# Eight experts in an order found on the chip, three of them with 64 token slots instead of 96

## What is computed

```
logits = h @ router_w + router_b
top_val, top_idx = top_k(logits, 2)          # two experts a token
combine = sum(one_hot(top_idx, 8) * softmax(top_val)[..., None], axis=-2)
for e in range(8):
    out = out + combine[..., e:e+1] * ((silu(h @ w1[e]) * (h @ w3[e])) @ w2[e])
```

## Time and profile before

| | us |
|---|---|
| median of 3 runs | 1945.97 (1945.91 to 1948.18) |
| span of the profiled execution, first to last instruction | 1944.6 |
| PE busy in the span | 1900.7 (98%) |
| matmuls of the expert stream, start of first and of last | 1023.8 and 1925.6 |
| the profiled execution's own time beside its span | the page gives none |

### The profile page before, as it was taken

How to read it: one execution, slowest core, us unless ns; L and a number is a source line. 1 busy time by engine, 2 the same in 40 slices (tenths; PEclk the granted TensorE clock), 3 DMA queues, 4 the chain that set the end, 5 groups by cost and what they waited for, 6 DMA issues and landing times.

```text
span 1944.6 us, 48442 instructions
## 1 busy us (share of the span) xinstructions
PE 1900.7 (98%) x22336; PEld 1386.6 (71%) x22337; DVE 603.1 (31%) x1194; ACT 449.6 (23%) x759; POOL 409.3 (21%) x126
## 2 busy tenths in 40 slices
PE   6999999999999999999999999999999999999997
PEld 4875888898888888968986666666666666666664
DVE  4355332253632545475541011110211111120112
ACT  4357322243222224465440000100000000000001
POOL 2400444435546454304530000000000000000000
PEclk8999999999999999999999999999999999999999
DMA  8352332226353655303589999999999999999990
GB/s 343 133 197 85 111 101 95 89 86 238 132 193 133 238 224 185 130 23 131 174 311 384 403 408 382 377 381 408 398 375 397 387 408 380 380 393 401 409 375 25
DMA packets 70144, 506.60 MB, mean 261 GB/s; under 512 B 7793, under 2 KB 8049, under 8 KB 9265
## 3 DMA queue, kind: packets, MB, share of 16 engines
q1 hardware_dynamic: 69552, 501.08, 66.3%
q0 software_dynamic: 384, 2.36, 0.3%
HBM read 502.36 MB, written 1.05 MB: 259 GB/s over the span
## 4 chain that ended last, share of the span: by engine, by line
PE 82%; issue 9%; POOL 5%; DMA 1%; DVE 1%; ACT 1%; SPq 0%; DVEq 0%; POOLq 0%; ACTq 0%
PE bank L1525 30%; PE bank L1537 14%; PE bank L937 10%; PE bank L939 10%; PE bank L938 10%; POOL w_lo L583 5%; DMA start_slab<-in_w_mod 1%; PE pv_bank L1288 1%; PE turned_pair L1270 1%; PE bank L972 1%; PE bank L1246 0%; PE bank L1539 0%; PE bank L1251 0%; PE turned_pair L1511 0%; PE bank L1511 0%
## 5 line engine op out<-in xcount | busy, mean ns | idle before, releaser
L1525 PE MATMUL bank<-moe_slab,HE 128*32 128x256 f32 x10752 | 592.8, 379 | 1.3 <-DVE GT L2847 1.3
L1525 PEld LDWEIGHTS bank<-moe_slab,HE 128*32 128x32 f32 x10752 | 348.7, 110 | 231.2 <-DVE GT L2847 1.8
L583 POOL TENSOR_TENSOR w_lo<-slab,w_hi 128x2048 fp32r<-128x2048 f32 (+3 forms) x88 | 369.0, 4196 | 540.3 <-ACT w_hi L1742 540.3
L937 PE MATMUL bank<-H_HI,w_hi 128*128 128x512 f32 (+1 forms) x912 | 321.6, 353 | 0.4 <-POOL H_LO L851 0.3
L938 PE MATMUL bank<-H_LO,w_hi 128*128 128x512 f32 (+1 forms) x912 | 319.6, 350 | 0.0
L939 PE MATMUL bank<-H_HI,w_lo 128*128 128x512 f32 (+1 forms) x912 | 319.5, 350 | 0.0
L1537 PE MATMUL bank<-moe_slab,GE 128*32 128x256 f32 x4032 | 299.8, 379 | 0.0
L1539 PE MATMUL bank<-moe_slab,GE 128*32 128x256 f32 x1344 | 299.1, 379 | 0.0
L1537 PEld LDWEIGHTS bank<-moe_slab,GE 128*32 128x32 f32 x4032 | 166.6, 110 | 115.0
L2844 DVE TENSOR_TENSOR GT<-SE,bank 128x256 f32<-128x256 f32 x56 | 23.6, 421 | 631.8 <-ACT SE L2082 631.8
L2080 ACT ACTIVATE SE<-bank 128x256 f32<-128x256 f32 x56 | 21.4, 383 | 772.0 <-PE bank L1525 772.0
(11 more groups left out here) (289 smaller groups left out, 2022.9 us busy)
## 6 DMA issues: line engine op xcount, KB each, us to landing
moe_slab<-in_moe_up SPq DMA_DIRECT2D x224, 1024.0 KB, 7.3
moe_slab<-in_moe_w SPq DMA_DIRECT2D x112, 1024.0 KB, 7.2
slab<-in_w_in SPq DMA_DIRECT2D x38, 1024.0 KB, 4.9
slab<-in_ffn_w SPq DMA_DIRECT2D x30, 1024.0 KB, 4.9
row_slab<-in_w_mod_rows SPq DMA_DIRECT2D x28, 1024.0 KB, 7.1
start_slab<-in_w_mod SPq DMA_DIRECT2D x8, 1024.0 KB, 17.1
slab<-in_w_proj SPq DMA_DIRECT2D x8, 1024.0 KB, 4.8
slab<-in_w_out SPq DMA_DIRECT2D x8, 1024.0 KB, 4.9
```

The costliest lines, as they stand in the source:

```text
L583: engine.tensor_tensor(lo, raw, hi.bitcast(F32), ALU.subtract).then_inc(done, 1)
L937: mm(out, lhs[0], rhs[0], start=start, stop=False)
L1525: ins = mm(outs[t // 2][32 * b:32 * b + 32, 256 * (t % 2):256 * (t % 2) + 256], rows[t], w[:, 256 * b:256 * b + 256], start=first and t != ...
```

## The change

On the chip the experts are ranked by their token counts (`order` on DVE, new; expert 0 always comes first, its key is set above all counts). Position p of the stream then takes the expert of rank `RANK_AT[p]`. Ranks 0 to 4 keep 96 slots, ranks 5 to 7 get 64; in counting from one, the positions with 64 slots are 2, 5 and 8. SP reads the expert of a position into a register and computes the addresses of its slabs from it. A position with 64 slots has matmuls for two groups of 32 tokens instead of three, with its own versions of the layout of the down product, the silu, the gate and the weighting. The gathers are five instead of four: position 1 alone right after `route`, then 2 and 3, 4 and 5, 6 and 7, and 8 alone, each from step 5 of positions 1, 3, 5 and 7. An expert with more tokens than its slots would go to the overflow passes. The ring, its 14 places, the order of slabs inside an expert and their 336 transfers stay.

```diff
+RANK_AT = (0, 5, 1, 2, 6, 3, 4, 7)
+WIDE = 5
+SLOTS_AT = [SLOTS if rank < WIDE else 64 for rank in RANK_AT]
+GATHERS = ((0,), (1, 2), (3, 4), (5, 6), (7,))
+PLACE_AT = (0, 1, 2, 0, 1, 2, 3, 0)
...
+            def expert_at(p):
+                sp.wait_ge(order_ready, 1)
+                return sp.value_load(ORDER[0:1, p:p + 1], min_val=0, max_val=N_EXPERTS - 1)
...
             def stream_load(k):
-                src, row = (a["moe_up"], (4 * n + i) * P) if kind == "up" else (a["moe_w2"], (2 * n + i) * P)
-                sp.dma_start(moe_slab[k % MOE_RING][:].rearrange("p k n -> p (k n)"), src[row:row + P, :])\
+                p, g = divmod(n, GROUPS)
+                src, each = (a["moe_up"], 4) if kind == "up" else (a["moe_w2"], 2)
+                row = (each * g + i) * P
+                if p:
+                    if p not in expert_of:
+                        expert_of[p] = expert_at(p)
+                    rows = src[bass.ds(expert_of[p] * (GROUPS * each * P) + row, P), :]
+                else:
+                    rows = src[row:row + P, :]
+                sp.dma_start(moe_slab[k % MOE_RING][:].rearrange("p k n -> p (k n)"), rows)\
...
             def token_groups(outs, rows, w, first, last):
-                for t in range(3):
+                for t in range(len(rows)):
...
+            def narrow_column_groups(out, rows, w, first, last):
+                for half in range(2):
+                    for q in range(4):
+                        b = 2 * half + q // 2
+                        ins = mm(out[32 * q:32 * q + 32, 256 * half:256 * half + 256], rows[q % 2],
+                                 w[:, 256 * b:256 * b + 256], start=first and half == 0, stop=last,
+                                 skip_group_check=True)
...
+            def order():
+                link(v.tensor_copy(KEY[:], COUNTF[:]))
+                link(v.memset(KEY[:, 0:1], 2.0 * S))
+                mine = KEY[:].unsqueeze(2).to_broadcast([P, 8, 8])
+                other = KEY[:].unsqueeze(1).to_broadcast([P, 8, 8])
...
+                placed(ORDERF[:], const("iota")[:, 0:8])
+                v.tensor_copy(ORDER[:], ORDERF[:]).then_inc(order_ready, 1)
+                placed(COUNT_AT[:], COUNTF[:])
...
+                for to, of in ((W_AT, W), (POS_AT, POS)):
+                    for t in range(2):
+                        placed(to[:, t, 0:8], of[:, t, 0:8])
...
             def stream():
                 for n in range(STEPS):
                     e, g = divmod(n, GROUPS)
-                    if e % 2 and e + 1 < N_EXPERTS and g == GATHER_AT:
+                    if n == 0:
+                        order()
+                    gather = next_gather(e) if g == GATHER_AT else None
+                    if gather:
```

More of the change, by code:

```diff
@@ L1561, in down_slab, with wait_tokens_out, scatter_quarter @@
                     k = 2 * i + kk
[L1562 to L1563 removed]
+                    first, last = g == 0 and k == 0, g == GROUPS - 1 and k == 3
+                    rows = [GE[:, n % 2, t, 32 * k:32 * k + 32] for t in range(groups)]
+                    if groups == 3:
+                        ins = column_groups(down, rows, w[:, kk, :], first, last)
+                    else:
+                        ins = narrow_column_groups(down[0], rows, w[:, kk, :], first, last)
                 ins.then_inc(slab_used, 1)
[L1566 to L1570 removed]
+            def wait_tokens_out(e, n, groups=3):
+                need = (1, 1, 2, 3) if groups == 3 else (1, 2, 2, 3)
+                pe.wait_ge(ytok_lo, 3 * e + need[n])
+            def scatter_quarter(n, out, slots=SLOTS):
                 for c in range(2):
                     col = P * (2 * n + c)
[L1573 to L1574 removed]
+                    mm(out[:, S * c:S * c + S], YTOK_HI[0:slots, col:col + P], SCATTER[0:slots], start=True,
+                       stop=False)
+                    ins = mm(out[:, S * c:S * c + S], YTOK_LO[0:slots, col:col + P], SCATTER[0:slots], start=False,
+                             stop=True)
                 ins.then_inc(scattered, 1)
@@ L2092, in token_high_parts, with narrow_token_high_parts @@
                 af(YTOK_HI[:, 768:1024], YLAST[:], ACT.Copy, scale=weight).then_inc(ytok_hi, 1)
+            def narrow_token_high_parts(e):
+                weight = SLOT_W[0:64, e % 2:e % 2 + 1]
+                hi = YTOK_HI[0:64, :].rearrange("p (a b n) -> p a b n", a=2, b=2)
+                act.wait_ge(slot_w_ready, e + 1)
+                af(hi[:, :, 0, :], down[0][0:64, :].rearrange("p (a n) -> p a n", a=2), ACT.Copy, scale=weight)\
+                    .then_inc(ytok_hi, 1)
+                for half in range(2):
+                    act.wait_ge(ylast_ready, 3 * e + 2 + half)
+                    af(hi[:, half, 1, :], YMOVED[:, 256 * half:256 * half + 256], ACT.Copy, scale=weight)\
+                        .then_inc(ytok_hi, 1)
             def last_token_high_parts():
@@ L3016, in constants @@
     put("pick", p[:, None] % 32 == f)
+    put("rank_at", np.array(RANK_AT)[None, :])
+    put("spare", SLOTS - np.array(SLOTS_AT)[None, :])
     put("fold", (p[:, None] // 64 == f // 2 % 2) & (p[:, None] % 32 == 2 * (f // 4) + f % 2))
```

174 lines of the change are left out of this document (119 added, 55 removed).

## The result

The changed kernel takes 1885.3 us in the median of 4 runs (1883.38 to 1887.5), against 1946.94 (1945.91 to 1948.18) for the kernel before on the same chip: a ratio of 0.9683, 95% interval 0.967 to 0.9697. The forecast of 1884 was right, in part by luck: two of its terms were off by some 5 us each and cancelled. The profiled execution took 1883.7 us with a span of 1881.9.

What follows compares the result with a forecast made beforehand. PE bounds the kernel, transfers close behind; from position 2 landings set the end: 1132.0 plus 284 x 2.57 = 729.9, last narrow slab 1.7, tail 18.6, sum 1882.2; plus 1.4, say 1884 us. Range 1856 to 1916.

Steps and rivals of the forecast that it cites:

- The bound: Whole stream: PE sets the pace before the change; with it, slabs land one behind the other from position 2 on.
- Narrow slabs: Positions 2, 5 and 8: 16 matmuls a slab instead of 24, so 1.73 us on PE instead of 2.59.
- Slabs landed at position 2: Start of position 2, about 1132.0: 54 slabs issued, two on the way, 52 landed, leaving 284 to land.
- The rate: Transfers from position 2 on: 2.57 us a slab, 408 GB/s, so 284 slabs take 729.9 us.
- The rival at the start's rate: Transfers from position 2 on run at 2.48 us a slab, as at the kernel's start: 1858 us; chance 0.16.
- PE's waits: Narrow positions 2, 5 and 8, most in the last two: PE waits some 47 us in all for landings.
- two wide positions put back some five of the 14 places: Wide positions between narrow ones: 43 to 45 slabs land in each while 42 are used; ring never full again.
- the transfers never rest: From position 2 to the end: transfers run without a pause, DMA share 1.00, no slice below 395 GB/s.
- The start: First gather, one expert instead of two, 96 columns per matmul instead of 192: 1.3 us gained.
- Ranking and addresses: Ranking on DVE, 5.5 to 7 us, hidden ahead of step 0's gate; SP's register addresses hidden: nothing for either.
- The tail: From the last matmuls to the end of the span: 18.6 us, with 1 us to either side.
- The clock rival: Narrow positions: PE's clock falls to 1.2 GHz, a narrow slab takes 3.45 us, up to 2055 in all; chance 0.03.

Runs made afterwards that it cites:

- e4: Changed kernel, but from position 2 on a down slab's transfer brings only its first half (512 KB), with the same matmuls: 1848.36 us, ratio 0.9495.
- e3: Changed kernel with 64 slots at all eight positions, tokens beyond an expert's 64th left out: 1869.05 us.
- e9: Changed kernel with the first gather taking position 1's tokens twice, 192 columns a matmul instead of 96: 1883.62 us, ratio 0.9678.
- e1: Changed kernel with constant slab addresses, experts in the order the ranking gives, instead of register addresses: 1884.96 us, ratio 0.9679.
- e7: Changed kernel with SP allowed to run only 7 slabs ahead of PE, not 14, the 14 places kept: 1912.21 us.
- e10: The changed kernel once more, unedited, beside the run with the wide first gather on one chip: 1888.83 us, ratio 0.9698.
- e6: Changed kernel with its three narrow positions moved from 2, 5 and 8 to 6, 7 and 8: 1908.62 us.
- e8: Changed kernel with 64 slots everywhere and the second group of 32 tokens multiplied only in the first up or down term: 1869.39 us.
- e2: Changed kernel with only positions 2 and 8 narrow, the fifth wide again: 1896.23 us, ratio 0.973.
- e5: Changed kernel with 96 slots at all eight positions; ranking, register addresses and five gathers stay: 1951.43 us, ratio 1.0024.

## Why the prediction was right, and where not

**The bound, shown.** PE paces the stream up to position 2 and the landings pace it from there to the end. e4 takes the landings away and PE's work ends 36.5 us earlier; e3 takes 181 us of PE's work away and the last landing comes 14.8 us earlier.

**Narrow slabs, right.** A wide slab is 48 matmuls and a narrow one 32 (the prediction counted half of each; the ratio of two thirds is what entered). In e4, where nothing waits, position 2 takes 78.5 us: 72.5 by the prediction, 2.4 for a scatter, and 4 x 0.86 = 3.4 because four of the up slabs in this stretch belong to the wide position behind it.

**Slabs landed at position 2: missed by two.** The step took 54 for issued and 52 for landed at 1132.0. In the trace 53 were issued by then and 50 had landed, the 50th at 1130.62 (the 287 slabs from 1132 in e4's expectation are one too many). I took two to be on the way; 7.3 us to landing over 2.59 us a slab already says nearly three. And PE came to position 2 at 1134.1, 2.1 us late, almost one slab.

**The rate: 2.57 us a slab came out nearly right, by two errors that cancel.** 286 slabs landed between 1130.62 and 1860.37: 2.552 us each. Two slabs more cost 5.1 us, 286 x 0.018 gave 5.1 back, and the 50th landing lay 1.4 us ahead of 1132.0: hence 1860.4 against 1861.9. The rate was read from windows with a share of 1.00, and it was still not the most that the transfers can do. In those windows some three slabs were outstanding, that is issued and not yet landed; with a deep queue they moved 419 to 420 GB/s at a share of 1.01. The rival at the start's rate was right that a deep queue moves more. At 419 GB/s a slab is 1.0486 / 0.419 = 2.50 us, and 286 of them would have ended 14 us earlier. They did not, because a slab has landed only with the last of its 16 parts, and eight parts run ahead of the others (last section): while 419 GB/s moved, slabs landed each 2.546 us (100th to 250th). The head start of the early parts comes back at the end: in the last 16 us 175 GB/s moved, which is 16 x (419 - 175) / 419 = 9.3 us, most of the 14. So 2.57 stood on a rate of the transfers that was too low and on no allowance for parts that land unevenly. Of the page of the Trainium skill that was weighed, "DMA: Bandwidth & Descriptors", Specifications: its 358 GB/s for a core, half of 716 for a pair of cores, is far below what every stretch of 1200 to 1650 us shows, where one core ran alone.

**PE's waits: 38 to 40 us, predicted 47.** They grow from position to position, as argued: 5.6, 14.2, 17.9. The forecast had PE's own work ending at 1817, against a last slab at 1863.6. e4 shows 1825.88: its first slab is 2.3 us behind that of the changed kernel, its position 1 is 1.3 us longer, and the changed kernel itself came to position 2 2.1 us late; the other 3 us are spread over the positions and were not split. The step said that two wide positions put back some five of the 14 places. They did: 6 slabs had landed and were not yet used at 1440, and 7 at most from position 3 on, at 1764, one of them in use; the kernel before holds 11 to 13. But the other places were taken too, by slabs on the way. So SP waits for PE in 1640 to 1780, 29 times before up slabs alone, and the transfers rest at 1740 to 1770, for about 30 x (419 - 395) / 419 = 1.7 us. Eight slabs were on the way there, but the parts that run ahead had only two or three left. That the transfers never rest was wrong by this much.

**The start: missed, and in sign.** I took 1.3 us gained. The gather of 96 columns starts a pair of matmuls each 0.22 us, as that of 192 does in e9's and the old trace, so half the columns gain nothing (in e1 and e7, where the clock holds, the first silu comes 14.34 us behind the gather's start, in the kernel before 14.38). It began 0.9 us earlier than before, and then the clock fell to half: the pair at 1022.35 takes 0.62 us instead of 0.39, and step 0's silu came at 1035.14, 0.7 us behind the 1034.43 of the kernel before. The term was 1.3 - (-0.7) = 2.0 us too good, which is nearly all of the 2.1 us by which position 2 came late.

**Ranking and addresses: nothing, right.** The ranking's last instruction ends at 1029.8 and DVE then idles for 6.05 us until the gate. For an address SP has a MOVE of 29 ns and register work of 46, and e1 and the changed kernel differ by 0.3 us.

**The tail: 19.6, predicted 18.6,** at the edge of its bounds. PE waits 1.41 us for `YTOK_LO` at 1864.82, behind the two copies in series that the prediction named without a price; the kernel before waits 0.62 there. In e1 and e10, which end their last slab within 1 us of the changed kernel, the tail takes 22.8: there the clock falls 3.8 us behind the last slab, in the changed kernel 13.3 us behind it. The prediction's 1 us to either side does not cover that. The end of the run lies 1.8 us behind the span, not 1.4.

**The clock rival** did not come in the profiled run. PE's granted clock is 1.00 from 1050 to 1850, in the narrow positions too, behind 48 waits of up to 1.4 us. In e10, the same kernel, it came once, for 3.4 us in position 2, behind a wait for a landing (a row of PE's timeline, and a window):

```profile
1209.92 2.73 PE L1572 MATMUL bank<-moe_slab,HE 128*32 128x256 f32 x32 [1.96 <-DMA moe_slab<-in_moe_up]
...
1210.90:1214.40 3.50, 3.50 (x40) 1.47 (x36) 0.87 (x2) 0.39 (x1) 0.00 (x0) 0.51 1.01 421
```

It did so once each in e3 and e6, behind waits of 2.01 and 2.15 us; ten other waits of over 1.9 us in e3, e6, e7, e9 and e10 were followed by no fall. The price was small: e10's last landing is at 1860.53, that of the changed kernel at 1860.37. In the Trainium skill, "TensorE: Matmul & The Clock Gate", the section on HAM oscillation has matmuls at half clock behind waits for transfers of some 3 to 5 us. No wait here is that long, so these runs do not test it. e8 shows that the clock falls often when PE has still less to do.

## What to carry to other kernels

When the bound engine is relieved, the time moves only as far as the next bound, and that one has to be priced at the pace at which whole slabs land under a deep queue. Neither the rate at a shallow queue (2.57 us a slab) nor that of the bytes at a deep one (2.50) is that pace (2.55). Light stages are worth most where they stand early and among heavy ones, so that a ring can refill and the transfers never rest: the same three narrow positions gave 23 us less at the end of the stream. A gather that gets smaller need not get shorter, and a fall of PE's clock in it can make the stage behind it start later than before.

## What the runs showed of the hardware

**A full DMA share has more than one rate.** With some three slabs of 1 MiB outstanding 402 to 410 GB/s moved at a share of 1.00 or 1.01, with eight to eleven 419 to 420 at 1.01, and in e7 with six 420. The number of slabs is not all: 395 moved with eight outstanding (1740 to 1770), and 405 with between six and seven on average in e2 (1450 to 1550). There the eight parts of a slab that run ahead had 2.4 and 3.2 slabs left on average, in the stretches of 418 to 420 about four and more. What the engines do in the time that a deeper queue saves, no run tells.

**SP's issue is held when the queue is long.** In the changed kernel and in e1 an issue takes up to 6.5 and 7.1 us, against 0.33 normally. In the trace this happens when 11 or 12 slabs are outstanding, the one being issued counted, and never are there more than 12, though the ring has 14. 12 x 2.55 = 30.6 us is also nearly the longest time to landing, 31.0. In e7 and e5, with at most seven and six outstanding, no issue takes over 0.71 us. The ring's last two places are not idle for that: in the wide positions they hold slabs that have landed, and SP waits for PE 60 times before slabs in 1300 to 1460 because all 14 are taken. What two places fewer would cost was not tried.

**Eight of sixteen parts of a slab land late.** Each slab signals 16 completions. In the trace of the changed kernel eight of them run ahead, and the time from the first to the last grows to between 14 and 19 us in the last 60 slabs; before the change it was 2.2 us in the median and 3.6 at most, and in e4, where the transfers rest, 2.5 and 6.0. PE's instruction fetches are a suspect: the stream has 113 of their packets in the changed kernel, 89 in e3 and 51 in e8, and the lag at the end is 16.5, 17.4 and 10.8 us. The lag falls with the fetches from e3 to e8, but not from the changed kernel to e3, so the cause stays open. Its price at the end of the changed kernel is the 9.3 us above; on average the 16 parts of the last slab land 8.6 us before its last one. In e3 that average is 8.3, in e8 5.1: 3.2 of the 4.3 us by which e8's last landing comes before e3's.

**PE's clock fell with PE hardly idle.** In the first gather, of 96 columns, the granted clock goes to 0.5, that is to 1.2 GHz, in eight of the ten traces that have it: for 3.4 us in the changed kernel, e2, e3, e6 and e10, for 6.8 in e4, e5 and e8. In e1 and e7 it holds 1.00, and so it does with 192 columns in the kernel before and in e9, at the same pace of 0.22 us a pair. Before the fall in the changed kernel PE had gone from 512 columns a matmul to 96, after an idle of 0.32 us. e9 has a fall of 3.4 us at 1735.55, at the end of its gather of 96 columns for position 8 and with no wait ahead of it; outside e8 no gather of 192 columns has one. From the start of the first gather to the first silu a wide position 1 takes 14.3 to 14.4 us without a fall, 16.0 with the short one and 17.6 with the long one, so a fall costs about half of its length. What decides whether it comes is open.
